# A fused float32 network on one core: sums for the fourth scan inside the second S5 output unit, a shared last copy of states, a later fetch of two weight sets

## The reference, cut to what matters

```python
ug = u.reshape(bsz, seq, S5_GROUPS, S5_GROUP)          # 64 groups of 16 channels
for direction in (0, 1):
    bu = einsum('sgc,gpc->sgp', us, bb[direction])     # complex, 64 states a group
    h  = associative_scan(h[t] = a * h[t-1] + bu[t], reverse=(direction == 1))
    y += einsum('sgp,gcp->sgc', h_re, c_re) - einsum('sgp,gcp->sgc', h_im, c_im)
z = gelu(y + d_skip * u)
return (z @ w_glu_a) * sigmoid(z @ w_glu_b)
```

## Time and profile before

| | us |
|---|---|
| median of 3 runs | 1170.21 |
| lowest and highest | 1169.49, 1174.09 |
| the profiled execution | 1172.47 |
| its span, first to last instruction | 1170.6 |
| TensorE busy | 1113.4 (95%) |
| VectorE busy | 829.1 (71%) |
| ScalarE busy | 558.1 (48%) |

### The profile page before, as it was taken

One profiled execution on the slowest core, in us unless ns is written; L12 is line 12 of the kernel. 1 busy time (PEld: TensorE's weight loads), 2 busy tenths in 40 slices (PEclk: granted clock), 3 DMA queues, 4 the chain that ended last, 5 costly groups with the idle time before them and its releaser, 6 DMA issues.

```text
span 1170.6 us, 21137 instructions
## 1 busy us (share of the span) xinstructions
PE 1113.4 (95%) x8970; PEld 971.9 (83%) x8970; DVE 829.1 (71%) x1414; ACT 558.1 (48%) x876; POOL 45.0 (4%) x71
## 2 busy tenths in 40 slices
PE   7899898999999997879999999999989999999998
PEld 4788676988888885469988888899978899988898
DVE  1699466877578674875677764578898966659955
ACT  3224633445101124653555543456677846467944
POOL 0010011000000000000000000000000000042000
PEclk9999998999999998999999999989999999999999
DMA  9977688899848957865455555525432345343342
GB/s 374 377 279 270 229 327 305 306 333 329 342 181 251 346 191 157 329 246 180 144 180 184 187 194 190 180 80 173 158 130 78 133 151 180 130 152 117 107 145 72
DMA packets 38287, 246.41 MB, mean 210 GB/s; under 512 B 4400, under 2 KB 5584, under 8 KB 9648
## 3 DMA queue, kind: packets, MB, share of 16 engines
q1 hardware_dynamic: 29072, 182.36, 45.8%
q0 software_dynamic: 6240, 43.94, 9.9%
q10 hardware_dynamic: 2880, 18.74, 3.9%
HBM read 225.24 MB, written 19.79 MB: 209 GB/s over the span
## 4 chain that ended last, share of the span: by engine, by line
PE 78%; DVE 10%; DMA 5%; ACT 4%; issue 2%; SPq 0%; ACTq 0%; DVEq 0%
PE ps L1494 11%; PE ps L1498 10%; PE ps L1496 10%; PE ps L1520 10%; PE ps L1501 10%; PE ps L1521 5%; PE ps L1645 4%; DMA ca_dram<-more 2%; PE ps L1738 1%; DMA more<-in_ada_w 1%; PE ps L2182 1%; PE ps L1593 1%; DVE ada_more L2974 1%; PE ps L1691 1%; PE ps L1871 1%
## 5 line engine op out<-in xcount | busy, mean ns | idle before, releaser
L1494 PE MATMUL ps<-rounded_parts,w_high_rounded 128*128 128x256 f32 x1136 | 328.9, 290 | 2.2 <-DVE rounded_parts L2335 1.3
L2328 DVE TENSOR_TENSOR ring_rounded<-ring,w_high_rounded 128x1024 fp32r<-128x1024 f32 x220 | 260.8, 1227 | 88.9 <-ACT w_high_rounded L882 88.5
L1496 PE MATMUL ps<-rounded_parts,w_high_rounded 128*128 128x256 f32 x1136 | 322.9, 284 | 0.0
L1498 PE MATMUL ps<-rounded_parts,ring_rounded 128*128 128x256 f32 x1136 | 322.8, 284 | 0.0
L882 ACT ACTIVATE w_high_rounded<-ring 128x1024 fp32r<-128x1024 f32 x220 | 219.8, 1049 | 63.8 <-PE ps L1521 48.2
L1494 PEld LDWEIGHTS ps<-rounded_parts,w_high_rounded 128*128 128x128 f32 x1136 | 219.6, 193 | 11.4 <-issue 6.7
L1496 PEld LDWEIGHTS ps<-rounded_parts,w_high_rounded 128*128 128x128 f32 x1136 | 219.6, 193 | 0.2
L1498 PEld LDWEIGHTS ps<-rounded_parts,ring_rounded 128*128 128x128 f32 x1136 | 219.4, 193 | 0.0
L1520 PE MATMUL ps<-rounded_parts,w_high_rounded 128*128 128x512 f32 x496 | 175.3, 399 | 0.0
L1521 PE MATMUL ps<-rounded_parts,ring_rounded 128*128 128x256 f32 x496 | 139.3, 281 | 0.0
L1501 PE MATMUL ps<-big,ring 128*128 128x256 f32 x544 | 121.0, 381 | 0.0
(11 more groups left out here) (426 smaller groups left out, 1555.1 us busy)
## 6 DMA issues: line engine op xcount, KB each, us to landing
ring<-in_blocks SPq DMA_DIRECT2D x139, 1024.0 KB, 4.9
ada_w<-in_ada_w POOLq DMA_DIRECT2D x27, 1024.0 KB, 7.5
ada_more<-in_ada_w POOLq DMA_DIRECT2D x13, 1024.0 KB, 7.5
we_dram<-we_t ACTq DMA_DIRECT2D x8, 1024.0 KB, 7.8
ca_dram<-more ACTq DMA_DIRECT2D x8, 1024.0 KB, 10.8
ring<-we_dram SPq DMA_DIRECT2D x8, 1024.0 KB, 5.7
ring<-ca_dram SPq DMA_DIRECT2D x8, 1024.0 KB, 7.2
big<-in_ada_w SPq DMA_DIRECT2D x4, 1024.0 KB, 11.3
```

What stands on the lines that cost most here:

```text
L1494: nc.tensor.matmul(out, high[:, k, columns], x_high, start=start, stop=False, skip_group_check=True)
L1496: nc.tensor.matmul(out, high[:, k, columns], x_low, start=False, stop=False, skip_group_check=True)
L1498: last = nc.tensor.matmul(out, low[:, k, columns], x_high, start=False, stop=stop, skip_group_check=True)
L2328: nc.vector.tensor_tensor(rounded(w), w, w_high[:, c % 2, ks], ALU.subtract)\
```

## The change

```diff
                 if name == "s5_in":
                     sp.dma_start(ring[:, b % RING].rearrange("p a b -> p (a b)"), we_dram[nb])\
                         .then_inc(w_here[b % RING], 16)
-                    if nb == RING - 1:
+                    if nb == RING + 1:
                         load_near(2)
                         load_near(3)
...
                 for ri in range(2):
-                    nc.scalar.activation(states[0:64, n % 2, ri, :, 1:NCH], turns_out[0:64, ri, :, 0:NCH - 1], ACT.Copy)
+                    ins = nc.scalar.activation(states[0:64, n % 2, ri, :, 1:NCH], turns_out[0:64, ri, :, 0:NCH - 1],
+                                               ACT.Copy)
+                    if n == 3:
+                        continue
                     ins = nc.scalar.activation(states[64:128, n % 2, ri, :, 0:NCH - 1][:, :, ::-1],
                                                turns_out[64:128, ri, :, 0:NCH - 1], ACT.Copy)
                 ins.then_inc(state_ready, 1)
...
             for n in range(4):
-                if n < 3:
+                if n < 2:
                     add_turns(n + 1)
                 if n == 2:
                     turn_z(0)
...
-                pe.wait_ge(state_ready, n + 1)
+                pe.wait_ge(state_ready, n + 1 if n < 3 else 5)
                 for a in range(4):
+                    if n == 1 and a == 2:
+                        add_turns(3)
...
+            dve.wait_ge(blocks_done, ready[first_unit["s5_out"] + 1])
+            for ri in range(2):
+                ins = nc.vector.tensor_copy(states[64:128, 1, ri, :, 0:NCH - 1][:, :, ::-1],
+                                            turns_out[64:128, ri, :, 0:NCH - 1])
+            ins.then_inc(state_ready, 1)
             for b in range(2):
                 dve.wait_ge(z_psum, b + 1)
```

## The result

The changed kernel takes 1175.22 us (median of 10 runs, 1172.99 to 1180.54) against 1170.56 us for the kernel before (10 runs on the same chip): ratio 1.0043, 95% interval 1.0026 to 1.0060, or 5.0 us slower (3.0 to 7.0). One of the runs of before took 1563.7 us; it is not counted in the ratio. The forecast was 1174.7 us.

The account below looks back on a forecast made before the run. Taken as bound by waits: TensorE's 5.71 us stall, then TensorE and VectorE passing work to and fro. Second scan +5.0 us, tail gain -0.45, sum +4.5 on 1170.21: 1174.7 us, range 1165 to 1179.

Parts of the forecast that it names:

- The stand: TensorE's idle at the scan stage's first products, read as an instruction fetch behind the near loads; all 5.71 us go.
- cover for later fetches: Later instruction fetches have some 10 us before TensorE runs out, so cost nothing; otherwise a stall up to 5.7 us.
- Its price: What the idle at the first input products costs: 5.71 us, taken off whole.
- rival 1: Near loads do not hold input block 6 back; the stage runs 5.71 us early: 1164.1 us; chance 0.14.
- Block 6: Input block behind the moved near loads lands at 482.6 us; its products began at 478.45 before.
- From that landing to the second scan: TensorE's work from input block 6's landing, partly at the lower clock: 9.8 us, second scan 5.0 us late.
- The sums: Sums moved inside the second output unit: fourth scan 15.3 us behind the second instead of 16.7, 1.4 us gained.
- The copy: Half the last state copy on VectorE: 1.2 us gone from ScalarE, VectorE's two copies taken at 0.6 us each.
- The tail: Fourth unit ends 3.6 us earlier, but the GLU block's landing lets its GELU gain 1.3; net 0.45 us.
- The 0.85 us for a lower clock in the turn of z: Turn of z behind the fourth unit, after 2.9 us idle, takes up to 0.85 us more.
- Rival 2: The idle at the first products stays and block 6 is still pushed: 1180.4 us; chance 0.08.
- Rival 3: The stage's end keeps its whole 3.6 us gain: 1171.6 us; chance 0.10.

Follow-up runs that it names:

- experiment 2: Changed kernel without the loads of near sets 2 and 3, ratio 0.9932; or with these sets issued behind input blocks 1 and 2, 0.9954.
- experiment 3: Kernel before with small transposes added near the start: 40, ratio 1.0034; 64, ratio 1.0014; 80, 1166.70 us in one run.
- the two splits: Near sets 2 and 3 issued behind input blocks 1 and 2, in the changed kernel, ratio 0.9954, and in the kernel before, 0.9946.
- fetch-only kernel: Kernel before with the two near sets issued behind input block 5 and nothing else: 1177.39 us, ratio 1.0045.
- experiment 5: Kernel before with only the sums moved, 1168.47 us, or only the last copy of states shared, 1167.52 us; one run each.
- experiment 1: Kernel before with only the later near-set fetch, ratio 1.0045; second kernel: changed kernel with that fetch line taken back, ratio 1.0001.
- experiments 2 and 6: Changed kernel without near loads, 0.9932, or near sets behind blocks 1 and 2, 0.9954; kernel before with only that split, 0.9946.
- order and copy alone: Changed kernel with near sets again issued behind input block 3, leaving the moved sums and shared copy: 1171.25 us, ratio 1.0001.
- experiment 4: Changed kernel with both near sets issued behind input block 2: 1164.22 us in one run.
- the split with the tail edits: Changed kernel with near set 2 issued behind input block 1 and set 3 behind block 2: 1166.56 us, ratio 0.9954.

## Why the prediction was right

**The stand.** Right, and shown: it is an instruction block of TensorE, fetched behind the near loads. It goes when the backlog goes (after, experiment 2) or when the boundary moves away (experiment 3). The Trainium skill, "Runtime: NRT & Kernel Launch", section Instruction fetch mechanics, has the next block fetched during the current one and mostly hidden; here it was not, at the one boundary with 2 MB queued ahead: 5.71 us. The forecast's "some 10 us" of cover for later fetches were hardly tried: in the kernel after one transfer came at 462.26 us, ahead of the near loads, and the next at 492.98, behind them and behind the new hole, when TensorE was at its record 8,211 (8,205 in the kernel without near loads). The nearest trial is the kernel with 80 transposes, whose transfer of 459.83 us came late and cost nothing. "DMA: Bandwidth & Descriptors", section Queues, rings and completion order, has the queues take turns; here the one packet on q8 started 8 us later than without the backlog (460.29 us, with near loads issued from 443.57 on and the last landing at 463.2), and at 461.49 and 459.13 us with 40 and 64 transposes, where q1 still had all 16 engines busy and its last near load landed 4 to 5 us later. So it need not wait for the whole backlog, but for much of it. That it waits is shown; why a single packet waits so long for its turn is not.

**Its price.** The term was 5.71 us; without near loads in the way the second scan comes 8 us earlier, not 5.71, and with the loads in place and the boundary moved away (80 transposes) 6.1. The lower clock behind the stand, which the forecast left out here, is the rest (experiment 2). This did not enter the forecast's result, because the new hole swallowed all of it: the start of block 6 was worked out from landings, not by subtraction. That the term was too small did no harm is in that sense luck; rival 1, which did subtract it, stood at -6.2 us, and the kernels in which it holds measured -8.0 (no near loads), -5.4 and -6.3 (the two splits).

**Block 6.** Forecast: its landing 25.75 us after the first input product. Measured: 486.89 - 461.23 = 25.66, and 25.2 in the fetch-only kernel. The near loads ended at +23.3 against 23.25.

**From that landing to the second scan.** Forecast 9.8 us, measured 9.03. Block 6 (1.94) and turn 5 (1.12) ran at the lower clock as said; block 7 took 1.26 us, not 1.93: the clock came back inside it, so the stretch shows 0.59. In the fetch-only kernel block 7 took 1.94 (488.85), as forecast. Thus the second scan was 4.1 us late instead of 5.0.

**The sums.** Forecast: fourth scan 15.3 us behind the second. Measured 15.35, with the sums running 3.67 us inside the second unit.

**The copy.** Two copies in 0.75 us on VectorE, where the forecast took 0.6 each, so this term was mis-sized without consequence; both engines end within 0.4 us of each other, and the wait before the fourth unit is gone. Its own waiting for the second unit showed nowhere.

**The tail.** Right in kind: the GLU block's landing binds, the GELU runs right behind ScalarE's roundings, the gain at the fourth unit is lost again but for 1.2 us, and 0.5 in three other kernels (experiment 5). The 0.85 us for a lower clock in the turn of z did not come in this execution: 1.09 us after 2.98 us of idleness. It came in experiment 1's second kernel, 1.97 us after 2.93:

```profile
513.17 1.97 PE L2005 MATMUL ps<-const,big 128*128 128x128 f32 x8 [2.93 <-ACT big L1185]
```

There the tail's gain was 0.5 us, the forecast's 0.45. Of the five kernels with both edits, three have the slow turn of z and two the fast one, so this term is a matter of the execution and not a fixed one.

**The sum.** Forecast +4.5. The two profiles give +2.9 in the stage, the timed runs +5.0 (3.0 to 7.0). Against the profile two terms are mis-sized, 0.9 us up to the second scan and 0.7 in the tail, most of both by the clock. In the kernels of experiment 1 the clock did as forecast, and the two parts alone show +4.1 (4.3 of it up to the second scan, where the landing came 0.5 us sooner than forecast) and, behind the second scan, -0.5. Which is usual in the timed runs is not known. The forecast's sum lies within their interval and the profile's, 2.9, just outside it, so some 2 us of the timed difference are not found in the one profiled execution, and that the total came out within 0.5 us is in part luck.

**The rivals.** Rival 1 (nothing holds block 6 back) fell with the 11.35 us, and its price shows in the kernels of experiments 2 and 6, where it is true. Rival 2 (the stand stays) fell with the unbroken 32 records. Rival 3 (the tail keeps 3.6 us) fell with the 2.63 us that ScalarE waits for the landing.

## What to carry to other kernels

A load's place in a queue is paid by everything behind it, and in this kernel by TensorE's instruction fetch on another queue too: where an engine stands still with "issue" as the reason, look for a backlog on the DMA engines and for a transfer of the instruction queue that comes late in it. Move such a load towards earlier slack and in portions, since later slack is often already promised: here two sets of 1 MB in two earlier places gained 0.5%, and the same sets two blocks later lost 0.4%. Before crediting two edits on one path with the sum of their gains, find the landing that caps both.

## What the runs showed that I had not expected

- The place of the stand follows the count of TensorE's records exactly: with 80 and 128 more records in front it stayed behind record 7,873, and so came that many records earlier in the work; 160 more removed it.
- Near loads that caused a stand of 5.71 us cost 8 us in all, 6.1 with the stand alone moved away.
- Either tail edit alone gained as much as both, and both gained less in three of five kernels.
- The granted clock after about 3 us without TensorE work is not the same from one execution to the next: it went to 0.50 after 2.64 us (before), 2.93 us (order and copy alone), 2.82 us (no near loads) and 2.87 us (experiment 4), and stayed at 1.00 over the next turn of z after 2.98 us (after) and 2.88 us (the split with the tail edits). In the last it fell just behind that turn; rows of its stretches:

```profile
513.00:514.20 1.20, 1.20 (x11) 1.20 (x12) 1.20 (x3) 0.07 (x1) 0.00 (x0) 1.00 1.00 416
514.20:516.00 1.80, 1.80 (x12) 1.80 (x10) 0.91 (x2) 1.77 (x3) 0.00 (x0) 0.52 1.04 432
```
